# Token sums loaded and rows stored by two issuing engines, and the root's table loaded at another place

## The chip, the cores and the metric
One core of one Trainium2 chip. The metric is the device time of one execution in microseconds (us), as the median of several runs; lower is better. One more execution was profiled.

## The reference
One layer of a hybrid diffusion backbone is applied to 128 context tokens and 512 latent tokens (640 rows of D = 1024 numbers, float32), then a last norm:

```python
h = rmsnorm(x, norm1_g) * (1 + sc1) + sh1
mix = token_mixers(h)                      # RWKV-7 scan, gMLP, depthwise conv, output projection
x = x + gt1 * mix
h = rmsnorm(x, norm2_g) * (1 + sc2) + sh2
x = x + gt2 * moe(h)                       # 16 experts, the best 2 of one group of 4 for each token
y = x * rsqrt(mean(x * x) + 1e-6) * final_g   # the last norm: y_prompt (128 rows), y_sample (512 rows)
```

The change touches only the last line and what stands around it. Outputs are y_prompt, y_sample and the scan states of the context.

## The kernel before
The 640 tokens are NT = 5 tiles of 128 rows. Tile 0 holds the context tokens, tiles 1 to 4 the latent ones. Each engine runs an instruction stream of its own, and they meet at semaphores that are written out by hand: `up(name, key)` adds to one, `at(name, key)` gives the value that it has after the step `key`. Without a key, `at` gives the value after the last step of that name in the whole program:

```python
def up(self, name, key=None, by=1):
    self.total[name] = self.total.get(name, 0) + by
    self.seen[(name, key)] = self.seen[(name, None)] = self.total[name]
def at(self, name, key=None):
    return self.sem(name), self.known[(name, key)] if self.known is not None else 1
```

`up16` is `up` by 16, which is what a whole DMA adds to its semaphore.

The experts work on up to 25 tiles of 128 gathered tokens. With the given inputs 18 of them are used. For each one PE multiplies with the expert's weights (L1719, L1742), ACT applies silu (L1349), DVE scales the result by the gate (L1606), and POOL adds its rows to the tensor `sum_rows` in DRAM with an indirect DMA (`add_rows`, L1275). From tile 13 on POOL waits for each addition to land and then raises `tile_added`. Tiles that aren't used are passed over by a branch on each engine (L1150 to L1159).

Then comes the end of the program, which is what the change is about, in `post_loads` (SP), `post_act` and `post_dve`:

- SP waits for the last `tile_added` and issues five loads of 512 KB, one for each token tile, from `sum_rows` to `x1` (L1212). Three semaphores count them, by `PICKS`: `sum_landed0` tile 0, `sum_landed1` tiles 1 and 2, `sum_landed2` tiles 3 and 4.
- ACT, for each tile in order 0 to 4: it waits for `at(PICKS[t])`, squares and sums the row (L1365, one ACTIVATE and one read of the accumulator), and takes the reciprocal root (L1368). The first L1368 needs a table that differs from silu's, so a table load stands in front of it.
- DVE multiplies the tile by that root and by `final_g` (L1628).
- SP stores the tile (L1216). POOL waits for all five stores (`stored`, L1310), and after that the engines drain and meet at the end of the block (rows of L67).

Of the kernel before, what the change touches and what calls it, by code (L numbers as in the profile page):

```python
# [6 lines left out]
ACT = mybir.ActivationFunctionType  # L7
# [5 lines left out]
P = 128  # L13


class Counts:
# [15 lines left out]
# [3 lines that stand above are left out]
        return self.sem(name), by  # L35

    def at(self, name, key=None):
        return self.sem(name), self.known[(name, key)] if self.known is not None else 1


def build(nc, A, outs, counts):
    D = 1024
    KD = D // P
    NT = 5
# [13 lines left out]
    up, at = counts.up, counts.at  # L58

    def up16(name, key=None):  # L60
        return up(name, key, 16)
# [5 lines left out]
    with ctx:  # L67
        counts.open(nc, ctx)

        def sb(name, shape, dt=F32):  # L70
            return ctx.enter_context(nc.sbuf_tensor(name, shape, dt))
# [19 lines left out]
        eps = sb("eps", [P, 4])  # L91
# [9 lines left out]
        rstd = sb("rstd", [P, 5, NT])  # L101
# [6 lines left out]
        def carve(n, at_=None):  # L108
            if at_ is not None:
                pos[0] = at_  # L110
            v = arena[:, pos[0]:pos[0] + n]
            pos[0] += n
            assert pos[0] <= AR, pos[0]
            return v
# [950 lines left out]
        x1 = carve(NT * D, at_=SCRATCH0).rearrange("p (t n) -> p t n", t=NT)  # L1065
# [55 lines left out]
        sum_dram = nc.dram_tensor("sum_rows", (T + P, D), F32).ap()  # L1121
# [39 lines left out]
        def each_tile(eng, used, i, step):  # L1161
            if ALWAYS <= i < SINGLES:
                if_used(eng, used, i, lambda: step(i))
            else:
                step(i)

        def tiles_used(eng):
            eng.wait_ge(*at("dve_did", "used"))
            return eng.value_load(used_i[0:1, :], min_val=0, max_val=CAP)

        def all_tiles(eng, run):

            used = tiles_used(eng)
            run(0, SINGLES, lambda i, step: each_tile(eng, used, i, step))
            if_used(eng, used, SINGLES, lambda: run(SINGLES, CAP, lambda i, step: step(i)))
# [7 lines left out]
        def post_loads(sp):  # L1183
            scan_done(sp)

            sp.wait_ge(*at("w_out_landed", "early"))
            sp.dma_start(wout[:, 5:8, :], A["w_out"][0].rearrange("(k p) n -> p k n", p=P)[:, 1:4, :]) \
                .then_inc(*up16("w_out_landed"))

            def spread(i):  # L1190

                for gi in range(2):
                    sp.dma_start(mods[:, i, gi, :], mod_dram[gi:gi + 1, i * D:(i + 1) * D].to_broadcast([P, D])) \
                        .then_inc(*up16("gate1_landed" if i == GATE1 else "mods_landed"))
            spread(GATE1)
            sp.dma_start(bc_row, A["norm2_g"].to_broadcast([P, D])).then_inc(*up16("vectors_landed"))
            sp.dma_start(wr_sb, A["w_router"].rearrange("(k p) e -> p k e", p=P)).then_inc(*up16("vectors_landed"))
            sp.dma_start(b_router_bc, A["b_router"].rearrange("(o e) -> o e", o=1).to_broadcast([P, NEXP])) \
                .then_inc(*up16("vectors_landed", "second norm"))
            for i in (SCALE2, SHIFT2, GATE2):  # L1200
                spread(i)
            for t in range(NT):
                sp.wait_ge(*at("dve_did", ("h2", t)))
                if t:
                    sp.wait_ge(*at("h2_stored", t - 1))
                sp.dma_start(sum_dram[t * P:(t + 1) * P, :], x1[:, t, :]).then_inc(*up16("sum_started"))
                sp.dma_start(h_dram[t * P:(t + 1) * P, :], h2[:, t % 2, :]).then_inc(*up16("h2_stored", t))
            sp.wait_ge(*at("dve_did", "scale2"))
            sp.dma_start(bc_row, A["final_g"].rearrange("(o e) -> o e", o=1).to_broadcast([P, D])).then_inc(*up16("vectors_landed"))
            sp.wait_ge(*at("tile_added"))  # L1210
            for t in range(NT):
                sp.dma_start(x1[:, t, :], sum_dram[t * P:(t + 1) * P, :]).then_inc(*up16(PICKS[t], t))  # L1212
            for t in range(NT):
                sp.wait_ge(*at("dve_did", ("out", t)))
                dst = outs[0][0] if t == 0 else outs[1][0, (t - 1) * P:t * P, :]
                sp.dma_start(dst, comb_rows[t]).then_inc(*up16("stored"))  # L1216


        rows12 = [wgu[:, s, 2 * i:2 * i + 2, :].rearrange("p k n -> p (k n)") for s in range(2) for i in range(4)] + \
            [wdn[:, s, i, :] for s in range(2) for i in range(2)]  # L1220
        comb_rows = rows12[0:NT]
        PICKS = [f"sum_landed{(t + 1) // 2}" for t in range(NT)]

        def post_pool(pool):
            g = nc.gpsimd
# [81 lines left out]
                        call(i - 1, add_rows)  # L1307
                call(end - 1, add_rows)
            all_tiles(pool, fetches)
            pool.wait_ge(*at("stored"))  # L1310

        def post_act(act):
            a = nc.scalar
            scan_done(act)
            for k, t in ORDER:
                if k == "turn_a":
                    act.wait_ge(*at("pe_did", ("turn_a", t)))
                    if t >= 2:
                        act.wait_ge(*at("pe_did", ("mix", t - 2)))
                    a.copy(catA[:, t % 2, :, :].rearrange("p k q -> p (k q)"), ps[5][:, :]).then_inc(*up("act_did", ("turn_a", t)))  # L1320
                elif k == "mix":
                    act.wait_ge(*at("dve_did", ("mix", t)))
                    if t >= 2:

                        act.wait_ge(*at("pe_did", ("turn_h2", t - 2)))
                        act.wait_ge(*at("h2_stored", t - 2))
                    a.activation(h2[:, t % 2, :], x1[:, t, :], ACT.Square, accum_out=sumsq[:, 0, t:t + 1]).then_inc(*up("act_did", ("square", t)))
                    act.wait_ge(*at("act_did", ("square", t)))
                    a.activation(rstd[:, 0, t:t + 1], sumsq[:, 0, t:t + 1], ACT.Abs_reciprocal_sqrt, bias=eps[:, 0:1],
                                 scale=1.0 / D).then_inc(*up("act_did", ("mix", t)))  # L1330
                elif k == "turn_h2":
                    act.wait_ge(*at("pe_did", ("turn_h2", t)))
                    if t:
                        act.wait_ge(*at("pe_did", ("router", t - 1)))
                    a.copy(h2T[:, 0:4, :].rearrange("p k q -> p (k q)"), ps[1][:, :]).then_inc(*up("act_did", ("h2", t)))
            act.wait_ge(*at("dve_did", "shifted"))
            a.activation(logit, logit, ACT.Exp).then_inc(*up("act_did", "exp"))

            def rows_half(i):
                act.wait_ge(*at("pe_did", ("turn_h", i)))  # L1340
                if i >= 2:
                    act.wait_ge(*at("pe_did", ("gu", i - 2)))
                a.copy(hT[:, i % 2, 0:4, :].rearrange("p k q -> p (k q)"), ps[0][:, :]).then_inc(*up("act_did", ("turn_h", i)))  # L1343

            def silu(i):
                act.wait_ge(*at("pe_did", ("gu", i)))
                if i:
                    act.wait_ge(*at("dve_did", ("gu", i - 1)))
                a.activation(act_in, ps[2 + i % 2][:, 0:DE], ACT.Silu).then_inc(*up("act_did", ("gu", i)))  # L1349

            def act_tiles(first, end, call):
                call(first, rows_half)
                call(first, silu)
                call(first + 1, rows_half)
                for i in range(first, end):
                    if i + 1 < end:
                        call(i + 1, silu)
                    if i + 2 < end:
                        call(i + 2, rows_half)
            all_tiles(act, act_tiles)  # L1360
            for t in range(NT):
                act.wait_ge(*at(PICKS[t]))
                if t:
                    act.wait_ge(*at("act_did", ("out_square", t - 1)))
                a.activation(mixed, x1[:, t, :], ACT.Square, accum_out=sumsq[:, 1, t:t + 1]) \  # L1365
                    .then_inc(*up("act_did", ("out_square", t)))
                act.wait_ge(*at("act_did", ("out_square", t)))
                a.activation(rstd[:, 1, t:t + 1], sumsq[:, 1, t:t + 1], ACT.Abs_reciprocal_sqrt, bias=eps[:, 0:1],  # L1368
                             scale=1.0 / D).then_inc(*up("act_did", ("out_rms", t)))

        def post_dve(dve):
            v = nc.vector
# [861 lines left out]
```

## Time and profile before

| | us |
|---|---|
| median of 3 runs | 995.33 (992.46 to 998.94) |
| time of the profiled execution | 989.59 |
| its span, first to last instruction | 987.9 |
| last silu starts (ACT) | 941.93 |
| first load of token sums issued (SP) | 965.53 |
| first Square of the last norm starts (ACT) | 969.01 |
| last DVE multiplication starts | 977.54 |

The span is what the trace covers. The profiled execution took 1.7 us more than its span, and the runs' median is 5.7 us above the profiled execution. ACT, DVE, PE, POOL and SP are the engines ScalarE, VectorE, TensorE, GpSimd and SyncE; a q behind the name (SPq, POOLq) is the engine's own sequencer, which issues DMAs and waits on semaphores.

### The profile page before, as it was taken

The numbers are of one execution on the slowest core, as the hardware profiler recorded it, in microseconds if no ns is written. First come the engines' busy times: TensorE is split into PE (matmuls) and PEld (weight loads), VectorE is DVE, ScalarE is ACT, GpSimd is POOL, SyncE is SP. The second block draws the span as 40 slices with busy tenths as digits, with TensorE's granted clock in tenths as the row PEclk, the third lists the DMA queues.
The fourth block names the chain that finished last, engine by engine and source line by source line (L and its number), as shares of the span: only waits on it lengthen the run. The fifth ranks groups of instructions, "written<-read, shape, count | busy, mean of one in ns | idle before, by whom it ended". The sixth has DMA issues, their size and how long they took to land. (4 is left out here: it accounts for less than half of the span.)

```text
span 987.9 us, 18024 instructions
## 1 busy us (share of the span) xinstructions
PE 794.0 (80%) x7510; PEld 494.6 (50%) x7510; DVE 500.2 (51%) x1054; ACT 264.1 (27%) x561; POOL 141.6 (14%) x136
## 2 busy tenths in 40 slices
PE   3699999999933819979699975999349999999940
PEld 2454456555521607767588752455334544444410
DVE  1400058656255898989999760433532333333322
ACT  2411014132235435656553620010100100000003
POOL 3000000000004130210310000000022333343220
PEclk9799999999965757979889986999559999999985
DMA  7952124244020000000000029321168999999845
GB/s 275 379 191 86 68 103 171 93 163 172 1 77 0 2 1 3 12 20 2 8 3 6 6 99 332 141 86 42 65 222 341 343 357 361 357 358 366 249 102 220
DMA packets 42329, 145.32 MB, mean 147 GB/s; under 512 B 5999, under 2 KB 8566, under 8 KB 37366
## 3 DMA queue, kind: packets, MB, share of 16 engines
q0 software_dynamic: 10368, 75.50, 22.2%
q1 hardware_dynamic: 31878, 68.63, 19.2%
q8 instruction: 62, 1.02, 0.4%
q14 instruction: 21, 0.17, 0.1%
HBM read 125.22 MB, written 19.43 MB: 146 GB/s over the span
## 5 line engine op out<-in xcount | busy, mean ns | idle before, releaser
L2176 PE MATMUL banks<-arena 128*128 128x512 f32 x304 | 155.7, 594 | 0.0
L1719 PE MATMUL banks<-arena 128*128 128x512 f32 x288 | 128.1, 598 | 1.1 <-ACT arena L1343 1.1
L2175 PEld LDWEIGHTS banks<-arena 128*128 128x128 f32 x304 | 57.2, 190 | 72.1 <-issue 70.3
L1719 PEld LDWEIGHTS banks<-arena 128*128 128x128 f32 x288 | 55.2, 192 | 70.3 <-issue 68.7
L1742 PE MATMUL banks<-arena 128*128 128x512 f32 x144 | 65.2, 595 | 1.6 <-DVEq L1159 1.6
L1591 DVE TENSOR_TENSOR arena<-arena,banks 128x256 f32<-128x256 f32 x18 | 7.6, 421 | 110.3 <-ACT arena L1349 104.5
L2055 DVE TENSOR_TENSOR arena<-arena 128x641 f32<-128x641 f32 x15 | 12.4, 827 | 99.6 <-ACT arena L1916 99.6
L2175 PE MATMUL banks<-arena 128*128 128x128 f32 x304 | 59.3, 277 | 1.6 <-ACT arena L201 1.6
L1349 ACT ACTIVATE arena<-banks 128x256 f32<-128x256 f32 x18 | 6.9, 384 | 179.5 <-PE banks L1719 179.5
L775 DVE TENSOR_TENSOR arena<-arena 128x30 f32<-128x30 f32 (+14 forms) x120 | 49.7, 414 | 4.1
L2045 DVE SCALAR_TENSOR_TENSOR arena<-arena 128x640 f32<-128x640 f32 x60 | 49.7, 876 | 0.0
L772 DVE TENSOR_TENSOR arena<-arena 128x30 f32<-128x30 f32 (+14 forms) x120 | 46.9, 391 | 2.7
L2176 PEld LDWEIGHTS banks<-arena 128*128 128x128 f32 x304 | 46.2, 192 | 0.0
L541 POOL MEMSET arena<- 128x2560 f32 x1 | 2.2, 2231 | 278.9 <-ACT catBC L211 278.9
L1606 DVE SCALAR_TENSOR_TENSOR arena<-banks,loraT,arena 128x512 f32<-128x512 f32 x36 | 25.4, 746 | 32.7 <-PE banks L1742 32.7
L1742 PEld LDWEIGHTS banks<-arena 128*128 128x128 f32 x144 | 26.1, 191 | 28.6 <-issue 25.8
L1255 POOL DMA_INDIRECT arena<-in_moe_w_gu_dram,loraT x18 | 17.2, 956 | 161.6 <-DVE arena L1551 115.1
L1652 PE MATMUL banks<-arena,catBC 128*128 128x512 f32 x80 | 36.7, 613 | 0.3 <-DVE rkvT L1398 0.3
L1652 PE MATMUL banks<-arena,rkvT 128*128 128x512 f32 x80 | 35.3, 594 | 0.0
L2159 PE MATMUL banks<-arena 128*128 128x512 f32 x80 | 34.5, 592 | 0.0
L1913 ACT ACTIVATE arena<-banks 128x128 f32<-128x128 f32 x15 | 4.2, 278 | 105.5 <-PE banks L2176 105.5
L1275 POOL DMA_INDIRECT sum_rows<-arena,loraT x18 | 29.0, 1609 | 21.1 <-DVE arena L1606 7.8
(349 smaller groups left out, 1490.0 us busy)
## 6 DMA issues: line engine op xcount, KB each, us to landing
arena<-in_ada_w_dram SPq DMA_DIRECT2D x12, 2048.0 KB, 12.3
arena<-in_w_in_dram SPq DMA_DIRECT2D x5, 2048.0 KB, 15.1
arena<-modulations SPq DMA_DIRECT2D x8, 512.0 KB, 8.1
sum_rows<-arena SPq DMA_DIRECT2D x5, 512.0 KB, 2.6
h_rows<-arena SPq DMA_DIRECT2D x5, 512.0 KB, 3.6
arena<-sum_rows SPq DMA_DIRECT2D x5, 512.0 KB, 5.5
out_dram<-arena SPq DMA_DIRECT2D x5, 512.0 KB, 2.6
arena<-in_x_sample_dram SPq DMA_DIRECT2D x4, 512.0 KB, 7.5
```

The lines of the kernel that those rows point to most:

```text
L772: v.tensor_tensor(t, vsub[:, j + 1:32, j:j + 1].to_broadcast([P, n, j]), vsub[:, j:j + 1, 0:j].to_broadcast([P, n, j]), ALU.mult).then_inc ...
L775: v.tensor_tensor(vsub[:, j + 1:32, 0:j], vsub[:, j + 1:32, 0:j], t, ALU.add).then_inc(*up("inverse_step", ("sub_add", m, j)))
L1255: g.indirect_dma_start(wgu[:, s, :, :].rearrange("p k n -> p (k n)"), None, wgu_rows, bass.IndirectOffsetOnAxis(ap=weight_u[:, i:i + 1], a ...
L1275: g.indirect_dma_start(sum_dram, bass.IndirectOffsetOnAxis(ap=sum_u[:, i:i + 1], axis=0), yrow[:, i % 2, :], None, compute_op=ALU.add).the ...
L1606: v.scalar_tensor_tensor(yrow[:, i % 2, cs], ps[5 + hf][:, :], slot_gate[:, i:i + 1], gate_row[:, i % 2, cs], ALU.mult, ALU.mult) \
L1652: x = T_.matmul(ps[6 + hf][:, :], lhs, wout[:, i, hf * 512:(hf + 1) * 512], start=(i == 0), stop=(i == KD - 1))
L1719: x = T_.matmul(ps[2 + s][:, :], hT[:, s, c, :], wgu[:, s, c, :], start=(c == 0), stop=(c == KD - 1))
L1742: x = T_.matmul(ps[5 + hf][:, :], actT[:, s, c * P:(c + 1) * P], wdn[:, s, c, hf * 512:(hf + 1) * 512], start=(c == 0), stop=(c == 1))
L2045: v.scalar_tensor_tensor(dst, src, ccol[:, 2 * k + c:2 * k + c + 1], dst, ALU.mult, ALU.add) \
L2159: x = T_.matmul(ps[2 + t % 2][:, :], h1T[:, k, t * P:(t + 1) * P], wslot(n)[:, k, :], start=(k == 0), stop=(k == KD - 1))
L2175: T_.matmul(ctx_[:, 0:P], w, h1T[:, k, 0:P], start=(k == 0), stop=(k == KD - 1))
L2176: x = T_.matmul(lat[:, :], w, h1T[:, k, P:T], start=(k == 0), stop=(k == KD - 1))
```

## The change
- The loads of tiles 0, 2 and 4 stay with SP. Those of tiles 1 and 3 are issued by ACT, which now waits for `tile_added` too. `SUMS` takes the place of `PICKS`: `sum_landed0` counts tiles 0, 2 and 4, `sum_landed1` counts tiles 1 and 3. The waits of ACT are `at(SUMS[t])`, again without a key.
- The stores of tiles 0, 2 and 4 stay with SP. ACT issues the store of tile 1 ahead of its Square of tile 4, and the store of tile 3 at the end. The semaphores are `stored0` and `stored1`; POOL waits for both, and SP waits for `stored1` at its end.
- Behind the last expert's silu ACT takes the reciprocal root of one small constant. It writes a column of `rstd` that is written again later, and it draws the table load to its place. Each L1368 gets a wait for that step.

```diff
             sp.wait_ge(*at("tile_added"))
-            for t in range(NT):
-                sp.dma_start(x1[:, t, :], sum_dram[t * P:(t + 1) * P, :]).then_inc(*up16(PICKS[t], t))
-            for t in range(NT):
-                sp.wait_ge(*at("dve_did", ("out", t)))
-                dst = outs[0][0] if t == 0 else outs[1][0, (t - 1) * P:t * P, :]
-                sp.dma_start(dst, comb_rows[t]).then_inc(*up16("stored"))
+            for t in (0, 2, 4):
+                sp.dma_start(x1[:, t, :], sum_dram[t * P:(t + 1) * P, :]).then_inc(*up16(SUMS[t], t))
+            for t in (0, 2, 4):
+                store_out(sp, t)
+            sp.wait_ge(*at("stored1"))
+
+        SUMS = [f"sum_landed{t % 2}" for t in range(NT)]
+
+        def store_out(eng, t):
+            eng.wait_ge(*at("dve_did", ("out", t)))
+            dst = outs[0][0] if t == 0 else outs[1][0, (t - 1) * P:t * P, :]
+            eng.dma_start(dst, comb_rows[t]).then_inc(*up16(f"stored{t % 2}"))
...
-        PICKS = [f"sum_landed{(t + 1) // 2}" for t in range(NT)]
...
-            pool.wait_ge(*at("stored"))
+            pool.wait_ge(*at("stored0"))
+            pool.wait_ge(*at("stored1"))
...
             all_tiles(act, act_tiles)
+            a.activation(rstd[:, 1, 0:1], eps[:, 0:1], ACT.Abs_reciprocal_sqrt, bias=eps[:, 0:1], scale=1.0).then_inc(*up("act_did", "table"))
+            act.wait_ge(*at("tile_added"))
+            for t in (1, 3):
+                a.dma_start(x1[:, t, :], sum_dram[t * P:(t + 1) * P, :]).then_inc(*up16(SUMS[t], t))
             for t in range(NT):
-                act.wait_ge(*at(PICKS[t]))
+                if t == 4:
+                    store_out(act, 1)
+                act.wait_ge(*at(SUMS[t]))
                 if t:
                     act.wait_ge(*at("act_did", ("out_square", t - 1)))
                 a.activation(mixed, x1[:, t, :], ACT.Square, accum_out=sumsq[:, 1, t:t + 1]) \
                     .then_inc(*up("act_did", ("out_square", t)))
+                act.wait_ge(*at("act_did", "table"))
                 act.wait_ge(*at("act_did", ("out_square", t)))
                 a.activation(rstd[:, 1, t:t + 1], sumsq[:, 1, t:t + 1], ACT.Abs_reciprocal_sqrt, bias=eps[:, 0:1],
                              scale=1.0 / D).then_inc(*up("act_did", ("out_rms", t)))
+            store_out(act, 3)
```

## Rows read from the trace of the kernel before

**Rows 1.** Chain that ended last, in order of time (start us, us, what)

```profile
965.53 0.32 SPq L1212
965.89 0.43 SPq L1212
966.37 5.55 DMA arena<-sum_rows
971.94 1.16 ACT rkvT L1365 x2
973.12 0.02 ACT rstd L1368
976.05 1.14 ACT rkvT L1365 x2
977.54 1.29 DVE arena L1628
```

**Rows 2.** Timeline of ACT from the last silu (start, us, idle before in brackets)

```profile
941.93 0.38 ACT L1349 ACTIVATE arena<-banks 128x256 f32<-128x256 f32 x1 [10.47 <-PE banks L1719]
969.01 1.06 ACT L1365 ACTIVATE rkvT<-arena 128x1024 f32<-128x1024 f32 x1 [26.70 <-DMA arena<-sum_rows]
969.97 0.19 ACT L1365 ACTIVATION_READ_ACCUMULATOR rkvT<-arena 128x1 f32 x1
970.18 1.28 ACT L1368 ACT_TABLE_LOAD   x1
971.47 0.29 ACT L1368 ACTIVATE rstd<-sum_squares,eps 128x1 f32<-128x1 f32 x1
971.94 1.06 ACT L1365 ACTIVATE rkvT<-arena 128x1024 f32<-128x1024 f32 x1 [0.17 <-DMA arena<-sum_rows]
...
974.68 1.04 ACT L1365 ACTIVATE rkvT<-arena 128x1024 f32<-128x1024 f32 x1
```

**Rows 3.** Source line L1212, the five loads of token sums

```profile
L1212 SPq DMA_DIRECT2D arena<-sum_rows x5: 319/432/452, 965.5 to 967.3; - x5
...
DMA to landing us min/median/max: 3.5/5.5/7.1
```

**Rows 4.** Source line L1216, the five stores of output rows

```profile
L1216 SPq DMA_DIRECT2D out_dram<-arena x5: 332/333/338, 973.2 to 978.9; - x5
...
DMA to landing us min/median/max: 2.6/2.6/2.7
```

**Rows 5.** Busy time by stretch; the last two columns: DMA share, GB/s

```profile
965.50:966.50 1.00, 0.00 (x0) 0.00 (x0) 0.00 (x0) 0.00 (x0) 0.00 (x0) 0.50 0.00 0
966.50:973.50 7.00, 0.00 (x0) 0.00 (x0) 1.34 (x2) 4.26 (x8) 0.00 (x0) 0.50 0.96 372
973.50:974.00 0.50, 0.00 (x0) 0.00 (x0) 0.50 (x1) 0.50 (x1) 0.00 (x0) 0.50 0.09 33
974.00:981.00 7.00, 0.00 (x0) 0.00 (x0) 4.59 (x4) 3.42 (x9) 0.00 (x0) 0.50 0.94 375
981.00:987.90 6.90, 0.00 (x0) 0.00 (x0) 0.00 (x0) 0.00 (x0) 0.00 (x0) 0.50 0.00 0
```

**Rows 6.** Timeline of DVE in the last norm

```profile
971.88 1.28 DVE L1628 SCALAR_TENSOR_TENSOR arena<-arena,rstd 128x1024 f32<-128x1024 f32 x1 [18.22 <-ACT rstd L1368]
973.45 5.38 DVE L1628 SCALAR_TENSOR_TENSOR arena<-arena,rstd 128x1024 f32<-128x1024 f32 x4 [0.28 <-ACT rstd L1368]
```

**Rows 7.** Source line L67, the end of the block

```profile
L67 POOLq EVENT_SEMAPHORE  x2: 17/17/17, 987.7 to 987.8; - x2
...
L67 POOLq COMPARE_BRANCH  x1: 38/38/38, 981.5 to 981.5; - x1
L67 POOLq DRAIN  x1: 5948/5948/5948, 981.7 to 981.7; - x1
```

**Rows 8.** Source line L1159 and timeline of POOL: the last addition and the skipped tiles

```profile
L1159 POOLq EVENT_SEMAPHORE  x2: 17/17/17, 965.2 to 965.5; - x2
...
958.74 1.56 POOL L1275 DMA_INDIRECT sum_rows<-arena,loraT  x1 [6.17 <-issue]
```

## The prediction
> **What bounds the kernel now.** The change touches only the end of the program, so I read the page just for its size and then went to the last 25 us. The timeline of POOL and the line of the skipped tiles come first: the last addition into the token sums is issued at 958.74, and POOL passes over the unused tiles at 965.2 to 965.5 [rows 8]. Nothing of the change acts before that moment, except a table load. From there the chain that ended last gives the order, and the reader should follow the clock times in it, not the shares: SP issues loads, the chain then hangs on one DMA from 966.37 to 971.92, then on ACT from 971.94 to 977.5, then on DVE to 978.83 [rows 1]. The last store is issued at 978.9 and lands 2.6 us later, at 981.5 [rows 4]; at 981.5 POOL leaves its wait, drains for 5.95 us, and the span ends [rows 7].
>
> The middle of this chain deserves a closer look. ACT squares tile 0 at 969.01, 3.5 us after its load was issued, which is the shortest of the five landings [rows 2, 3]. It then loads a table, takes the root by 971.76, and starts on tile 1 at 971.94, released by a DMA 0.17 us after it came free [rows 2]. That DMA is the third load: issued at 966.37, landed 5.55 us later at 971.92 [rows 1], and 5.5 is the median landing [rows 3]. Tile 1's Square had waited for tile 2 as well, because tiles 1 and 2 share a semaphore and `at(PICKS[t])` has no key, so it asks for that semaphore's final value. This is the fact on which my forecast rests: ACT waits for all loads of a semaphore, not for its own tile. The last load is issued at 967.3 and lands after 7.1 us, at 974.4 [rows 3], before ACT gets to tile 3 at 974.68 [rows 2], so it costs nothing now. From tile 1 on ACT works without a break: 971.94 to 974.68 is two tiles, **1.37 us a tile**, and DVE's four multiplications in 5.38 us keep the same pace [rows 2, 6].
>
> **The loads and their semaphores.** The new `sum_landed0` counts tiles 0, 2 and 4. ACT's first wait, `at(SUMS[0])`, therefore asks for all three. In the kernel before, tile 0 had a semaphore to itself. So I need the time at which the last of tiles 0, 2 and 4 has landed. All five loads together are 5 x 512 KB = 2.62 MB. They begin to move 1 us after the first issue and keep the DMA engines at a share of 0.96 and 372 GB/s from 966.5 to 973.5; then the share falls to 0.09 [rows 5]. The engines are full, so a second issuing engine can only save time in which they stand idle, a few tenths at the start. SP took 2.24 us to issue five (965.53 to 967.3 plus 0.45) [rows 1, 3], and the new order has the fifth issued by about 966.4, but the data still need those 7 us. Tile 4 is the last that SP issues, and SP has more bytes than ACT (1.57 against 1.05 MB), so I take the semaphore of the even tiles as the last to be full: **974.4**, the landing of the fifth load now. The bounds are 974.0 (the start is 0.4 us earlier, one issue) and 974.9 (two streams cost some efficiency, 7% of 7 us, as between the 0.96 of rows 5 and a share of 0.89).
>
> The page "DMA: Bandwidth & Descriptors" of the Trainium skill says, under "Queues, rings and completion order", that each DMA engine goes round-robin between the queues it has work for, a packet at a time. No run here shows two such queues yet. By that rule ACT's two tiles would be complete first and SP's three at the end, as I took it.
>
> **The sum on the path.** Now ACT goes into its steady work at tile 1, at 971.94, with four tiles to go. After the change it goes into it at tile 0, at 974.4, with five to go. That is 974.4 - 971.94 = **+2.46** and one more tile, **+1.37**.
>
> **The store inside ACT's stream.** Ahead of tile 4's Square stands the store of tile 1. Its wait is for DVE's tile 1, done 1.37 + 1.5 + 1.29 = 4.2 us after ACT began (a root starts 1.18 after its Square and DVE 0.33 after that; 1.28 for the multiplication [rows 1, 6]); ACT gets there after 5.3 us, so it doesn't wait. The issue itself takes 0.33 us on SP [rows 4] and 0.32 to 0.45 for a load [rows 3]; there is no row of one on ACT. Queued behind it are tile 4's Square, its root, DVE's last multiplication and the last store, all on the path. Bounds: 0, if the issue runs beside the 0.29 us root [rows 2], and 0.9, twice the longest on SP. I take **+0.3**, SP's own price for a store.
>
> **The loads on ACT** are issued while ACT has nothing else to do (it is idle for 26.7 us ahead of tile 0 [rows 2]), so their 0.4 to 0.9 us cost nothing against a landing 8 us later. Without that cover each would be 0.45. **The store of tile 3** is issued by ACT after its last root; DVE has tile 3 ready by then, its data pass ahead of tile 4's, and it can't end last. It isn't taken off the path either: SP now has three stores with issues of 0.33 us, and each was issued as soon as DVE was done (973.2, the first, is 0.03 after DVE's end), so the stores of before weren't queued [rows 4, 6]. Gain 0. The last one still costs DVE's end plus 2.6. SP's added wait for `stored1` has nothing behind it, and POOL's second wait asks for stores that land earlier.
>
> **The table load.** 1.28 us leave the stretch between tile 0's Square and its root [rows 2] and go into the 26.7 us of idle time ahead of it, hidden. In the kernel before it lies beside the landing of tile 2: without it ACT would be free at 970.5 and wait for the same 971.92. So in the old order of landings its removal is worth nothing. In the new order it would lie on the path, with all loads landed; moving it saves what the change would otherwise add. Either way the term against the time of before is 0. The page "ScalarE: Activation LUTs" of the Trainium skill, under "What ACT_TABLE_LOAD costs", gives 1283 ns plus a drain of about 1380 ns for each switch, 2.66 us. The trace agrees on the load and shows no drain around it: the accumulator was read until 970.16, the load starts at 970.18 and the root at 971.47 [rows 2]. By the page the rows would sit differently, and by neither would the path of before become shorter, since even then only the first root would be earlier.
>
> **Behind DVE** nothing changes: 2.6 us to land and POOL's 5.95 us drain [rows 4, 7]. Sum: 2.46 + 1.37 + 0.3 = **+4.1 us**. Against the profiled execution that is a span of 987.9 + 4.1 = 992.0 and 993.7 for its time; the median of the runs lies 5.7 us above the profiled one, for reasons that don't lie in this stretch, so against it I forecast 995.33 + 4.1 = **999.4 us**.
>
> **Rivals.**
> (a) The even tiles land ahead of the odd ones, because ACT leaves its wait or issues later than SP and its data queue up behind. Then tile 0 is squared early, but tile 1 waits for the odd tiles at 974.4, since the same 2.62 MB must have moved. Four tiles remain from there: 2.46 + 0.3 = +2.8, with the 974.0 bound +2.4, so about 998. For it: SP has always issued alone, nothing shows how the two share. Against: both wait for one event and SP's issues take 0.4 us apiece. 12 in 100.
> (b) The drain of POOL absorbs the delay: its 5.95 us might end at a moment that was set earlier (work of its queue since the last addition at 958.74) and not a fixed time after 981.7. Then the drain would be 1.8 us long, the span stays at 987.9, and the time at 995.3: not slower. It decides if the drain is under 5 us in the trace after. For it: the drain is long, and no engine or DMA is busy in it (share 0.00 [rows 5]). Against: it starts 23 us after POOL's last DMA. 6 in 100.
> (c) The change does what its words say, a gain: two queues bring all data sooner. To break even by this alone, all five must land by 974.4 - 4.1 = 970.3, that is 2.62 MB in the 3 us from 966.5 with 0.8 us for the last completion: 0.9 TB/s against 372 GB/s at a share of 0.96 [rows 5]. If instead each tile could be used as it landed (a wait for its own load only), ACT would start tile 0 at 969.0, have no table load, take tile 1 at 970.4, tile 2 at its landing at 971.9, and so tile 4 at 974.7 and not at 976.05 [rows 1]: 1.35 us earlier than now, 994.0. The missing key in `at` speaks against it. 3 in 100.
> (d) ACT is a poor host for DMAs: the issue of a store in its stream drains it or takes over a microsecond. Each microsecond is one on the path; with 2.5 us it is +6.3, about 1001.7. 9 in 100.
> The forecast itself has 70 in 100.
>
> **How the numbers follow.** The mechanism's bounds are 2.4 (rival a at its low bound) and 974.9 - 971.94 + 1.37 + 0.9 = 5.2, or 997.7 to 1000.5. The runs of one kernel spread over 6.5 us (992.46 to 998.94), more than the effect, so a median of a few may be off by 2 to 3 us in each of the two kernels, and that adds to both sides: 994.5 to 1003.5, which takes in (a), (b) and (d). Within 1% (9.95 us) is about what a measurement can tell from no change. No case reaches it alone; only (d) with a high draw of the runs would be slower by more: 5 in 100. Faster by over 1% has no mechanism: 1 in 100. The rest, 94 in 100, is within 1%.
>
> **What the profile after would show.** ACT's first Square of the last norm starts near 974.4, over 8.5 us after the first load is issued (3.5 now), and the other four follow at 1.37 us with no DMA wait between them. A table load stands at about 943 and none between Square and root. The DMA share is still near 1 for 7 us behind the first issue. There is a gap of some 0.3 us more ahead of tile 4's Square. The last store is issued near 983.0, and POOL's drain is again 5.9 us. Wrong would be a first Square at 969 to 971 (the wait isn't for the whole semaphore), an issue on ACT of over 1 us, or a drain that has shrunk by what the rest has grown.

## The result and the profile after

The changed kernel takes 1000.88 us (median of 22 runs) against 995.10 us (22 runs of the kernel before): a ratio of 1.0053 with a 95% interval of 1.0032 to 1.0074, so 3.2 to 7.4 us slower. The forecast was 999.4, +4.1. The forecast range, 994.5 to 1003.5, also holds the 995.33 of no change at all, so the time by itself can't tell whether the mechanism was right. The profiled execution took 998.48 us, with a span of 996.6.

One run differs from the next by more than the effect, and much of that arises ahead of the changed code: the first load of token sums is issued at 965.53 in the profile before and at 969.26 in the one after, though nothing that changed stands ahead of it but one hidden step on ACT. So I compare the **tail**, from the issue of that first load to the end of the span: 987.9 - 965.53 = 22.4 us before, 996.6 - 969.26 = 27.3 us after, **+5.0 us** (worked out before rounding).

The chain that ended last, in the kernel after (it answers to [rows 1]):

```profile
969.26 0.32 SPq L1212
969.62 0.43 SPq L1212
970.10 8.04 DMA arena<-sum_rows
978.16 1.16 ACT rkvT L1377 x2
...
983.98 0.11 ACTq L1222
984.09 0.04 issue
984.13 0.02 ACTq L1376
984.14 0.04 issue
984.19 1.16 ACT rkvT L1377 x2
985.76 1.28 DVE arena L1642
```

The DMA that the chain hangs on is now SP's third load, tile 4, and its landing comes 8.04 us behind its issue at 970.10. ACT starts its first Square at 978.16, 8.90 us after the first issue, where its steady work began 6.41 us after it before. The chain also shows ACT's own DMA issue (L1222) just ahead of tile 4's Square. The timeline of ACT after, to set beside [rows 2]:

```profile
945.45 1.28 ACT L1367 ACT_TABLE_LOAD   x1 [0.59 <-ACTq L1159]
946.74 0.29 ACT L1367 ACTIVATE rstd<-eps 128x1 f32<-128x1 f32 x1
969.26 0.83 ACTq L1370 DMA_DIRECT2D arena<-sum_rows  x2
978.16 1.06 ACT L1377 ACTIVATE rkvT<-arena 128x1024 f32<-128x1024 f32 x1 [31.12 <-DMA arena<-sum_rows]
979.12 0.19 ACT L1377 ACTIVATION_READ_ACCUMULATOR rkvT<-arena 128x1 f32 x1
979.40 0.29 ACT L1381 ACTIVATE rstd<-sum_squares,eps 128x1 f32<-128x1 f32 x1
979.60 1.04 ACT L1377 ACTIVATE rkvT<-arena 128x1024 f32<-128x1024 f32 x1
...
982.46 1.04 ACT L1377 ACTIVATE rkvT<-arena 128x1024 f32<-128x1024 f32 x1
...
983.71 0.38 ACTq L1222 DMA_DIRECT2D out_dram<-arena  x1
984.19 1.06 ACT L1377 ACTIVATE rkvT<-arena 128x1024 f32<-128x1024 f32 x1 [0.21 <-ACT rstd L1381]
```

The table load is gone from the path, and no wait for a DMA stands between the five Squares. But they come 1.43 or 1.44 us apart and not 1.37, and the last comes 1.73 behind the fourth. The busy time of stretches after (columns as in [rows 5]; the last two are DMA share and GB/s), beside [rows 5]:

```profile
970.30:977.50 7.20, 0.00 (x0) 0.00 (x0) 0.00 (x0) 0.00 (x0) 0.00 (x0) 0.50 0.95 360
977.50:981.50 4.00, 0.00 (x0) 0.00 (x0) 1.63 (x2) 3.15 (x7) 0.00 (x0) 0.50 0.00 0
981.50:984.50 3.00, 0.00 (x0) 0.00 (x0) 2.72 (x3) 2.61 (x7) 0.00 (x0) 0.50 0.44 175
984.50:989.80 5.30, 0.00 (x0) 0.00 (x0) 2.08 (x2) 1.13 (x3) 0.00 (x0) 0.50 1.00 396
```

First the loads run with all compute engines idle, then ACT and DVE run with the DMA engines idle for 4 us, and then four stores stand in line. In the kernel before, ACT and DVE had 4.26 and 1.34 us of work inside the 7 us of the loads [rows 5]. The last store of the kernel after, and the end of the block (they answer to [rows 4, 7]):

```profile
L1222 SPq DMA_DIRECT2D out_dram<-arena x1: 333/333/333, 987.1 to 987.1; - x1
...
DMA to landing us min/median/max: 3.2/3.2/3.2
```

```profile
L67 POOLq COMPARE_BRANCH  x1: 38/38/38, 990.3 to 990.3; - x1
L67 POOLq DRAIN  x1: 5948/5948/5948, 990.5 to 990.5; - x1
```

The last store takes 3.2 us to land and not 2.6; POOL's drain is 5.95 us as before. DVE's last multiplication ends at 978.83 before and at 987.04 after, and POOL leaves its wait at 981.5 and 990.3. The +5.0 us, term by term:

| | before | after | difference |
|---|---|---|---|
| first issue to the start of ACT's unbroken work | 6.41 (Square of tile 1) | 8.90 (tile 0) | +2.5 |
| from there to DVE's last multiplication | 5.60 (four Squares) | 7.60 (five) | +2.0 |
| DVE's end to the end of POOL's wait | 2.7 | 3.2 | +0.55 |
| rest to the end of the span | 6.4 | 6.3 | 0 |

### The profile page after: what moved, and what is told of

It reads as the page before. It is cut to its first block and busy times, and to the rows that moved or that the text cites. A ratio compares the mean times of both kernels' runs of the same rounds, so it can differ in the third digit from the quotient of the medians.

```text
span 996.6 us, 18032 instructions
## 1 busy us (share of the span) xinstructions
PE 794.7 (80%) x7510; PEld 494.5 (50%) x7510; DVE 500.5 (50%) x1054; ACT 264.6 (27%) x562; POOL 141.5 (14%) x136
## 5 line engine op out<-in xcount | busy, mean ns | idle before, releaser
L1280 POOL DMA_INDIRECT sum_rows<-arena,loraT x18 | 29.0, 1609 | 22.4 <-issue 14.6
```

Of the source, the lines that this page charges most:

```text
L1280: g.indirect_dma_start(sum_dram, bass.IndirectOffsetOnAxis(ap=sum_u[:, i:i + 1], axis=0), yrow[:, i % 2, :], None, compute_op=ALU.add).the ...
```

## The experiments

Two theories were set against each other. **W**: ACT waits for the whole of a semaphore, and the new grouping puts the last tile on the first one. **Q**: two issuing engines slow the loads. Smaller questions were added for each remaining term. "Square" gives the start of each of the five Squares after the first load's issue, and all rows are of profiled executions, one of each kernel. e2, e3, e5, e6 and e8 ran only that once, so for them the trace is all there is. How far a tail can be trusted is seen from parts that no edit touched: with SP alone the first load lands 3.4 to 3.7 us after its issue (before, e1, e3, e7, e8) and the last load 8.5 to 9.4 us after the first issue. Differences of up to 0.4 us between two tails are therefore not told apart by themselves; smaller terms are read from the spacing inside one trace.

| kernel | Square 0 ... 4, us | tail, us |
|---|---|---|
| before | 3.48, 6.41, 7.79, 9.15, 10.52 | 22.4 |
| after | 8.90, 10.34, 11.77, 13.20, 14.93 | 27.3 |
| e1 SP alone, two groups | 8.83, 11.49, 12.86, 14.22, 15.59 | 27.4 |
| e2 both queues, old groups | 4.92, 7.58, 8.95, 10.31, 11.68 | 23.5 |
| e3 before, table early | 3.77, 6.82, 8.20, 9.57, 10.93 | 22.7 |
| e4 after, own semaphores | 4.82, 6.27, 7.69, 9.12, 10.85 | 23.3 |
| e5 after, stores on SP | 8.66, 10.11, 11.54, 12.96, 14.39 | 26.2 |
| e6 after, one table wait | 8.73, 10.11, 11.48, 12.84, 14.49 | 27.0 |
| e7 before, table early, own semaphores | 3.79, 5.17, 6.54, 7.90, 9.27 | 21.5 |
| e8 before, own semaphores | 3.39, 6.05, 7.42, 8.78, 10.15 | 22.0 |

### e1: the grouping without the second queue

```diff
-        PICKS = [f"sum_landed{(t + 1) // 2}" for t in range(NT)]
+        PICKS = [f"sum_landed{t % 2}" for t in range(NT)]
```

> The kernel before with one edit: the semaphores of the five loads are grouped as in the change (even tiles, odd tiles). SP alone issues, the table load stays where it was. The measure is the tail, from the issue of the first load of token sums to the end of the span: 22.4 us in the kernel before, 27.3 after. Theory W (ACT waits for the whole of a semaphore): the first Square waits for tile 4 and starts 8.9 us after the first issue, then the table load (1.28) lies open in front of the first root: Square 1 at about 11.5 after the issue where it was 6.4, so a tail of 27.5 us and a time 5 us above before. Rival Q (two issuing engines slow the loads): SP alone is as before, tail 22.4 and first Square at 3.5.

Measured: tail 27.4 us; 1000.42 us (12 runs) against 997.03 (29 runs of before), ratio 1.0036 (1.0005 to 1.0068). ACT's timeline:

```profile
980.07 1.06 ACT L1365 ACTIVATE rkvT<-arena 128x1024 f32<-128x1024 f32 x1 [32.78 <-DMA arena<-sum_rows]
981.03 0.19 ACT L1365 ACTIVATION_READ_ACCUMULATOR rkvT<-arena 128x1 f32 x1
981.23 1.28 ACT L1368 ACT_TABLE_LOAD   x1
982.53 0.29 ACT L1368 ACTIVATE rstd<-sum_squares,eps 128x1 f32<-128x1 f32 x1
982.73 1.04 ACT L1365 ACTIVATE rkvT<-arena 128x1024 f32<-128x1024 f32 x1
```

One line of the program, with no second queue, brings a delay as large as that of the whole change: the first Square waits 8.83 us, as in the kernel after (8.90). W holds, and Q is not needed for that wait. With every load landed the table load lies in the open and costs 2.66 - 1.37 = 1.29 us between Square 0 and 1; this is what its move saves in the kernel after. That the two tails agree (27.4 and 27.3) is partly chance: in e1 this 1.29 us stands where the kernel after has other costs, which e5 and e6 measure below.

### e2: the second queue without the grouping

```diff
-            for t in range(NT):
+            for t in (0, 2, 4):
                 sp.dma_start(x1[:, t, :], sum_dram[t * P:(t + 1) * P, :]).then_inc(*up16(PICKS[t], t))
...
             all_tiles(act, act_tiles)
+            act.wait_ge(*at("tile_added"))
+            for t in (1, 3):
+                a.dma_start(x1[:, t, :], sum_dram[t * P:(t + 1) * P, :]).then_inc(*up16(PICKS[t], t))
```

> The kernel before with the loads of tiles 1 and 3 issued by ACT, the old semaphore groups (0; 1 and 2; 3 and 4), the table load and the stores as before. Theory W: tile 0 now lands at 4.9 after the first issue (as in the trace after) and not at 3.5, the table load ends near 7.3, tile 2 lands at 7.3, so Square 1 starts at 7.6 to 7.8 where it was 6.4: tail 23.7 us. Rival Q: the delay of the change is here whole, tail 26 us or more.

Measured: tail 23.5 us, +1.1; Square 0 at 4.92. ACT's timeline:

```profile
978.41 1.06 ACT L1368 ACTIVATE rkvT<-arena 128x1024 f32<-128x1024 f32 x1 [28.47 <-DMA arena<-sum_rows]
979.37 0.19 ACT L1368 ACTIVATION_READ_ACCUMULATOR rkvT<-arena 128x1 f32 x1
979.57 1.28 ACT L1371 ACT_TABLE_LOAD   x1
```

Square 1 stands at 7.58, right behind the root of tile 0. So two queues have a price, though a small one and not as Q put it: tile 0 lands 4.9 us after the first issue, 1.4 us later than before, and tile 1 at 5.1, so the two shared the DMA engines from the start, while the last tile lands at 8.9 as before.

### e4: the changed kernel with a semaphore for each load

```diff
-        SUMS = [f"sum_landed{t % 2}" for t in range(NT)]
+        SUMS = ["sum_landed0", "sum_landed1"] + [f"ring_landed{i}" for i in range(3)]
```

(The key of `up16` becomes `("sum", t)`, so that it doesn't meet the ring's own keys; the same in e7 and e8.)

> The changed kernel with one semaphore for each load (three of them are old ones of the weight ring whose earlier uses are long done), all else as changed. Theory W: the first Square starts with tile 0's landing, 4.9 us after the first issue, tile 4's Square at 4.9 + 4 x 1.43 + 0.3 = 10.9 where it was 14.9 in the changed kernel, tail 23.3 us, 1 us above before. Rival Q: the tail stays at 27.3.

Measured: tail 23.3 us; 995.88 us (10 runs) against 997.03, ratio 0.9989 (0.9955 to 1.0023).

```profile
977.53 1.06 ACT L1377 ACTIVATE rkvT<-arena 128x1024 f32<-128x1024 f32 x1 [28.11 <-DMA arena<-sum_rows]
...
978.98 1.04 ACT L1377 ACTIVATE rkvT<-arena 128x1024 f32<-128x1024 f32 x1
```

Both queues, the split stores and the early table stay, and 4.0 of the 5.0 us are gone. This is W from the other side. What is left, a tail 0.9 us longer than before, is a last Square 0.3 us later (10.85 against 10.52) and a last store that lands after 3.2 us and not 2.6: even where each tile is used as it lands, the split over two queues, with its added waits and its line of stores, brings no gain.

### e3 and e8: the table load and the semaphores, each alone

```diff
             all_tiles(act, act_tiles)
+            a.activation(rstd[:, 1, 0:1], eps[:, 0:1], ACT.Abs_reciprocal_sqrt, bias=eps[:, 0:1], scale=1.0).then_inc(*up("act_did", "table"))
+            act.wait_ge(*at("act_did", "table"))
```

> The kernel before with the table load alone moved behind the last silu. My prediction put its worth at 0 beside the old loads, since Square 1 then waits for tile 2's landing, 6.4 us after the first issue, with or without it: tail 22.4 us, Square 1 at 6.4. Rival: the table load lay on the path, tail 21.1.

Measured: tail 22.7 us, Square 1 at 6.82 where 6.4 was expected. ACT's timeline:

```profile
972.48 1.06 ACT L1367 ACTIVATE rkvT<-arena 128x1024 f32<-128x1024 f32 x1 [25.07 <-DMA arena<-sum_rows]
...
973.66 0.29 ACT L1370 ACTIVATE rstd<-sum_squares,eps 128x1 f32<-128x1 f32 x1
975.53 1.06 ACT L1367 ACTIVATE rkvT<-arena 128x1024 f32<-128x1024 f32 x1 [1.57 <-DMA arena<-sum_rows]
```

The 1.28 us of the table load have become 1.57 us of waiting for a DMA. Moved alone it brings nothing. The loads of this execution also landed 0.2 to 0.4 us later than in the profile before (Square 0 at 3.77, not 3.48), which is the tail's 0.3. Now e8, only the semaphores (the `PICKS` line as the `SUMS` line in e4):

> The kernel before with one semaphore for each load and nothing else. The table load now stands between tile 0's Square (3.5) and its root, whose end at 6.2 after the first issue lets Square 1 start at 6.25 to 6.4: tail 22.2 to 22.4 us. Only together with the moved table load do own semaphores bring more (21.0 expected).

Measured: tail 22.0 us, a little below the 22.2 to 22.4 expected and 0.4 below before, which two tails alone don't tell apart. Square 1 at 6.05 (6.25 to 6.4 was expected) comes 2.66 us behind Square 0, the same spacing as in e1: the table load is then what holds it. Before, the table load and the shared semaphore lay side by side, and each hid nearly all of the other.

### e5 and e6: the smaller terms

e5 stores all tiles from SP and takes `store_out(act, 1)` and `store_out(act, 3)` out of ACT's stream. All five stores count on one semaphore `stored` again, as before, and POOL waits for it alone.

```diff
-            for t in (0, 2, 4):
+            for t in range(NT):
                 store_out(sp, t)
-            sp.wait_ge(*at("stored1"))
...
-                if t == 4:
-                    store_out(act, 1)
...
-            store_out(act, 3)
```

> The changed kernel with all five stores back on SP, loads and table as changed. In the trace after, tile 4's Square comes 1.73 us behind tile 3's where the others are 1.43 apart, and the last store took 3.2 us to land where it took 2.6 before. Theory S (ACT holds back tile 1's store until tile 3's root, and four stores then stand in line on the same DMA engines): both go, the gap is 1.43, the landing 2.6, tail 27.3 - 0.3 - 0.6 = 26.4 us. Rival (the late landing has another cause): 27.0.

Measured: tail 26.2 us, Squares 3 and 4 are 1.43 apart, and the landings of the five stores are short again:

```profile
DMA to landing us min/median/max: 2.6/2.7/2.7
```

Both halves of theory S hold: 0.3 us for the issue in ACT's stream and 0.5 us for the line of stores. (The other 0.2 us of the tail's 1.1 is a first Square at 8.66 and not 8.90, which the edit doesn't explain.) In the kernel after DVE had tile 1 ready at 982.45, 4.29 us behind ACT's start, but ACT issued its store at 983.71, beside SP's store of tile 2 at 983.9. The four stores from then on take 1.3 us each (512 KB at 396 GB/s), and the last stands behind the others.

e6 waits for the table step once:

```diff
+            act.wait_ge(*at("act_did", "table"))
             act.wait_ge(*at("tile_added"))
...
-                act.wait_ge(*at("act_did", "table"))
                 act.wait_ge(*at("act_did", ("out_square", t)))
```

> The changed kernel with the wait for the table step once, ahead of ACT's loads, and not ahead of each root. In the trace after, Squares are 1.43 us apart where they were 1.37 before. If the added wait is the cause, the pace is 1.37 again and the tail 27.3 - 0.3 = 27.0 us; if it is something else the pace stays at 1.43.

Measured: Squares 1.36 to 1.38 apart and 1.65 ahead of the last, tail 27.0 us. The root starts 1.18 us behind its Square, as before, where it started 1.24 behind in the kernel after. The chain of the kernel after shows why: with two waits ahead of the root, one stands as an instruction of its own between the read of the accumulator and the root, and it is in neither before nor e6.

```profile
979.32 0.02 issue
979.34 0.02 ACTq L1380
979.35 0.05 issue
979.40 0.04 ACT rstd L1381
```

A second wait that is long satisfied costs 0.06 us each time, 0.3 us on a path of five. The spacing shows this, and not the tail: of the tail's difference 0.17 us is a first Square that came earlier (8.73, not 8.90).

### e7: both edits together

The kernel before with e3's and e8's edits together.

> The kernel before with one semaphore for each load and the table load behind the last silu; SP alone issues all loads and stores. Theory W with the landings of before (3.5, 4.7, 6.4, 7.7 and 8.9 us after the first issue): Squares start at 3.5, 4.9, 6.4, 7.8 and 9.1 where the last was 10.5, so a tail of 21.0 us, 1.4 less than before and 6.3 less than after. A theory in which something else than the Squares' start sets the end (DVE's pace of 1.29, stores that queue) gives 22 us or more.

Measured: Squares nearly as expected (3.79 to 9.27, 1.25 us earlier at the last), but a tail of 21.5 us, only 0.9 below before and between theory (21.0) and rival (22 or more). It is 994.00 us (12 runs) against 997.03, ratio 0.9978 (0.9949 to 1.0006): by the device time not told apart from before, by the tail of its one trace the shortest of all ten kernels. The missing 0.5 us is the rival's part: the stores, by the line L1216 and the stretches of this run (last two columns DMA share and GB/s):

```profile
DMA to landing us min/median/max: 3.0/3.2/3.4
```

```profile
974.80:981.80 7.00, 0.00 (x0) 0.00 (x0) 2.57 (x2) 4.11 (x10) 0.00 (x0) 0.50 0.96 369
981.80:984.80 3.00, 0.00 (x0) 0.00 (x0) 2.81 (x3) 2.67 (x6) 0.00 (x0) 0.50 1.02 416
984.80:988.30 3.50, 0.00 (x0) 0.00 (x0) 1.05 (x1) 0.00 (x0) 0.00 (x0) 0.50 0.98 396
```

The first store is issued at 980.5, while the loads still run, and from there the DMA engines have no gap up to 988.3: 5.2 MB in 13.5 us. All five stores land after 3.0 to 3.4 us where it was 2.6 to 2.7 in the kernel before. ACT's pace has been replaced as the bound by the DMA engines. They have no idle time left from the first load to the last store that earlier compute could fill; that only fewer bytes would shorten this further is argued from that and wasn't tried.

## Why the prediction was right

- **The loads and their semaphores** (974.4, or 8.9 us after the first issue): right. ACT started 8.90 us after it, and e1 and e4 show the cause from both sides. The last load landed 8.9 us after the first issue in either kernel, so a second issuing engine saved nothing. The page "DMA: Bandwidth & Descriptors" of the Trainium skill says under "Issuing engines are not separate DMA queues" that DMAs issued by different engines run on the same 16 DMA engines, and that only the time on the issuing sequencer is saved. The trace agrees: the fifth load was issued 0.84 us behind the first and not 1.8, and landed no earlier. The landings of the kernel after, first SP's line, then ACT's:

```profile
L1212 SPq DMA_DIRECT2D arena<-sum_rows x3: 320/432/433, 969.3 to 970.1; - x3
...
DMA to landing us min/median/max: 4.9/7.0/8.0
```

```profile
L1370 ACTq DMA_DIRECT2D arena<-sum_rows x2: 353/402/450, 969.3 to 969.6; - x2
...
DMA to landing us min/median/max: 5.1/6.3/7.6
```

- **The sum on the path** (+2.46 + 1.37): +2.5 and one more tile, as forecast.
- **The added wait for the table step: missed.** The part on the table load put the whole edit at 0 and said nothing of the wait ahead of each root. It cost 0.06 us for each of five tiles, 0.3 in all (e6: Squares 1.37 apart again), so the pace forecast for the profile after, 1.37 us a tile, came out at 1.43.
- **The store inside ACT's stream** (+0.3): right; 0.30 us in the gap, and ACT's issues take 0.35 to 0.45 us, like SP's. e5 removes it.
- **"It can't end last"**, of ACT's stores: true of tile 3's, but the step looked only at whether each store was ready, and took 2.6 us for the last. Tile 1's store, held back by 1.3 us in ACT's stream (ready at 982.45, issued at 983.71), made a line of four. The term is +0.55 where I had 0. With the missed wait this is the 0.9 us between +4.1 and +5.0. The median moved by 5.8; its interval, 3.2 to 7.4, takes in both sums, so it is the tail that finds the two misses.
- **The table load** (0 against before): right. e3 turns it into a wait for a DMA. In the open it is worth 1.29 us (e1, e2 and e8), so the page "ScalarE: Activation LUTs" of the Trainium skill, "What ACT_TABLE_LOAD costs", with its 2.66 us for a switch, doesn't hold at this place: the switch adds the load's 1.28 us and no more. (The 2.66 us between Squares 0 and 1 in these runs is another thing: a whole tile of 1.37 and the load.)
- **Rivals.** (a) fell: SP's last tile landed at 978.1, ACT's at 977.2 (969.6 + 7.6). (b) fell: the drain is 5948 ns in both kernels. (d) fell: an issue on ACT takes 0.45 us at most. (c) fell: the change brought no gain. Its condition, a wait for each load alone, gave a gain only without the second queue: with SP alone (e7) the tail is shorter than before by 0.9 us, of the 1.35 that I gave it, since the stores then meet the end of the loads; with both queues (e4) it is longer by 0.9, since tile 0 lands at 4.8 and not at the 3.5 that I had kept from the old loads, and the added waits and the line of stores stay.

## What to carry to other kernels

Before you regroup loads under shared semaphores, ask what value the consumer waits for: a wait for a shared semaphore's final value makes its first consumer wait for its last load. What removed the wait here was a semaphore for each load; a wait for a lower value of the shared one was not tried. Where the DMA engines are already full, as here (share 0.96), don't expect splitting a stream of loads over two queues to help: the last tile landed no sooner and the first one later. And of two costs that lie side by side, such as a table load and a shared semaphore here, removing one may bring next to nothing; measure them together.

## What the runs showed of the hardware

- With two queues the two first loads shared the DMA engines from the start. Tile 0 landed 4.7 to 4.9 us after its issue (after, e2, e4, e5) where it landed at 3.4 to 3.7 with SP alone (before, e1, e3, e7, e8). In e6, where ACT's first issue came 0.06 us behind SP's, it was 4.2. The last load landed 8.6 to 8.9 us after the first issue with two queues and 8.5 to 9.4 with one.
- A second wait ahead of ACT's root, whose condition had long been met, cost 0.06 us on a chain of dependent instructions (after against e6).
- POOL's drain at the end of the block took 5948 ns in all ten profiles, whatever the tail ahead of it.
- Most of the difference between runs goes with TensorE's granted clock, and TensorE does nothing in the tail (PE busy 0.00), so it lies outside the changed code: among the 22 runs of the changed kernel the three fastest (995.62 to 996.47 us) had a mean granted clock of 0.883 to 0.888 and the three slowest (1007.71 to 1009.38 us) one of 0.870 to 0.874. For a change of this size at the end of a program the trace's tail decides, and the median only agrees.
